# The Mixer's first levels issued ahead of its attention, whose 24 steps begin one in each slot

## The reference, cut to what matters

```
# differential attention: 6 heads, 4 blocks of 128 queries each: 24 steps
s = q_blk @ k^T  (two maps m of 32 channels);  p = softmax(s - slope * |i - j|)
a = p[0] - lam * p[1];   o = a @ v;   lam = exp(lq1 . lk1) - exp(lq2 . lk2) + lambda_init

# gated delta rule: 6 heads, both directions, chunks of 64 tokens
solve (I + strict_lower(kb k^T * decay)) [u, w] = [v*beta, kb*exp(gc)]
for each chunk:  v_new = u_i - w_i @ S;  o = qg_i @ S + aqk_i @ v_new
                 S = S * gl_i + kdec_i^T @ v_new
```

## Time and profile before

| what | value |
|---|---|
| median of 3 runs | 3787.8 us (3787.16 to 3788.26) |
| the profiled execution | 3787.34 us |
| its span on the core | 3785.6 us |
| TensorE busy | 3650.9 us, 96% |
| VectorE, ScalarE, GpSimd busy | 57%, 41%, 9% |
| granted clock of TensorE, mean | 0.986 |

### The profile page before, as it was taken

How to read it: one execution, slowest core, us unless ns; L and a number is a source line. 1 busy time by engine, 2 the same in 40 slices (tenths; PEclk the granted TensorE clock), 3 DMA queues, 4 the chain that set the end, 5 groups by cost and what they waited for, 6 DMA issues and landing times. The chain is left out here.

```text
span 3785.6 us, 58644 instructions
## 1 busy us (share of the span) xinstructions
PE 3650.9 (96%) x24913; PEld 3014.9 (80%) x24913; DVE 2164.9 (57%) x3353; ACT 1537.3 (41%) x2423; POOL 337.5 (9%) x325
## 2 busy tenths in 40 slices
PE   7999899999999999999999998999999999999998
PEld 4887688888888888878888776777888777778887
DVE  4734766455466444474227766745377866644375
ACT  3224632111354322253226435643266436633364
POOL 0030220000000000000000005510000014400000
PEclk9999899999999999999999998999999999999999
DMA  5530013333212111122223311013232311022231
GB/s 194 179 105 5 7 46 112 123 123 123 86 62 78 64 56 54 65 89 89 92 86 100 102 45 43 19 47 99 87 103 89 91 51 26 19 83 84 89 101 67
DMA packets 262767, 301.24 MB, mean 80 GB/s; under 512 B 9371, under 2 KB 229426, under 8 KB 262514
## 3 DMA queue, kind: packets, MB, share of 16 engines
q1 hardware_dynamic: 260433, 293.41, 24.2%
q10 hardware_dynamic: 2080, 4.19, 0.3%
HBM read 284.14 MB, written 2.10 MB: 76 GB/s over the span
## 5 line engine op out<-in xcount | busy, mean ns | idle before, releaser
L536 PE MATMUL banks<-h_halves,w_halves 128*128 128x512 f32 x3708 | 1370.4, 370 | 14.2 <-DVEq L428 10.6
L538 PE MATMUL banks<-h_halves,w_halves 128*128 128x512 f32 x3708 | 1364.7, 368 | 0.0
L540 PE MATMUL banks<-h_halves,w_halves 128*128 128x512 f32 x3708 | 1359.5, 367 | 0.0
L536 PEld LDWEIGHTS banks<-h_halves,w_halves 128*128 128x128 f32 x3708 | 699.0, 189 | 146.3 <-issue 13.9
L540 PEld LDWEIGHTS banks<-h_halves,w_halves 128*128 128x128 f32 x3708 | 697.3, 188 | 119.2
L538 PEld LDWEIGHTS banks<-h_halves,w_halves 128*128 128x128 f32 x3708 | 698.6, 188 | 115.6 <-issue 1.4
L263 DVE TENSOR_TENSOR w_halves<-work,w_halves 128x2048 fp32r<-128x2048 f32 (+1 forms) x212 | 482.8, 2277 | 484.9 <-ACT w_halves L258 484.9
L258 ACT ACTIVATE w_halves<-work 128x2048 fp32r<-128x2048 f32 (+1 forms) x212 | 401.8, 1895 | 387.1 <-PE banks L540 363.4
L258 ACT ACTIVATE h_halves<-kept 128x512 fp32r<-128x512 f32 (+1 forms) x520 | 332.9, 666 | 281.4 <-PE banks L540 235.6
L263 DVE TENSOR_TENSOR h_halves<-kept,h_halves 128x512 fp32r<-128x512 f32 (+1 forms) x514 | 356.9, 736 | 137.0 <-ACT h_halves L258 135.8
L1130 DVE SCALAR_TENSOR_TENSOR kept<-kept 128x512 f32<-128x512 f32 x280 | 189.8, 751 | 10.3 <-DMA kept<-in_mod_w 10.3
(11 more groups left out here) (415 smaller groups left out, 4693.0 us busy)
## 6 DMA issues: line engine op xcount, KB each, us to landing
work<-in_w_ff SPq DMA_DIRECT2D x64, 1024.0 KB, 5.3
work<-in_ffn_w_in SPq DMA_DIRECT2D x44, 1024.0 KB, 5.0
kept<-in_mod_w SPq DMA_DIRECT2D x40, 1024.0 KB, 5.2
work<-in_odd_w_in SPq DMA_DIRECT2D x24, 1024.0 KB, 5.2
work<-in_w_in SPq DMA_DIRECT2D x24, 1024.0 KB, 5.2
work<-in_ffn_w_out SPq DMA_DIRECT2D x16, 1024.0 KB, 5.2
work<-in_even_w_in SPq DMA_DIRECT2D x13, 1024.0 KB, 5.4
work<-in_odd_w_out SPq DMA_DIRECT2D x8, 1024.0 KB, 5.1
```

The lines of the kernel that those rows point to most:

```text
L536: nc.tensor.matmul(o, low[:, k - a, fc], rh[:, tc], start=opens, stop=False, skip_group_check=shared)
L538: nc.tensor.matmul(o, high[:, k - a, fc], rl[:, tc], start=False, stop=False, skip_group_check=shared)
L540: mm = nc.tensor.matmul(o, high[:, k - a, fc], rh[:, tc], start=False, stop=(k == K - 1), skip_group_check=shared)
```

## The change

The list `begins` holds the slot in which each step starts: 2, 3, ... 25, one a slot. So lags 0 to 4 of five steps stand in one slot, from slot 6 to 25; the last `weigh` is in slot 29. `scores(0)`, its wait for the stack and the 14 holds behind it go from ahead of TensorE's loop; 4 holds come into each of slots 1 to 4. In TensorE's `attend` and in ScalarE's loop the work of the older step (`weigh`, `out`) now comes ahead of that of the younger one (`turn_step` part 0, its copy). On VectorE `lambdas` and the memsets come ahead of `update(0, 0)`, and `query_gram(0)`, `lambdas_difference` and `queries(0, d)` move from ahead of the loop into slots 1, 2 and 3. `results_of_states` moves from level 5 to level 6, except in the last seven slots.

```diff
+    begins = [2 + s for s in range(N)]
+
     def step_at(t, lag):
 
-        s, odd = divmod(t + 2 - lag, 2)
-        return s if odd == 0 and 0 <= s < N else None
+        return begins.index(t - lag) if t - lag in begins else None
...
-                    if lv == 5:
+                    if lv == (6 if h < H else 5):
                         results_of_states(h - 1)
...
                 if place == 0:
-                    for s, work in ((step_at(t, 3), lambda s: turn_step(s, 0)), (step_at(t, 4), weigh)):
+                    for s, work in ((step_at(t, 4), weigh), (step_at(t, 3), lambda s: turn_step(s, 0))):
...
             pe.wait_ge(v_copied, 3)
-            pe.wait_ge(loads_in, 96)
-            scores(0)
-            core.hold(7, 14)
...
+                    if 0 < t < 5:
+                        core.hold(7, 4)
                     if h < H and lv:
                         products(h, lv)
...
-            exps(0)
             for t in range(slots):
...
                     rescale(step_at(t, 2))
+                if step_at(t, 4) is not None:
+                    out(step_at(t, 4))
                 if step_at(t, 3) is not None:
                     copy(step_at(t, 3), 0)
-                if step_at(t, 4) is not None:
-                    out(step_at(t, 4))
...
-            update(0, 0)
             dve.wait_ge(loads_in, 96)
             lambdas()
             for u in pl.u:
                 nc.vector.memset(c4(u[HD:P, 0:512])[:, :, 0:HD], 0.0)
                 nc.vector.memset(c4(u[0:HD, 512:1024])[:, :, HD:P], 0.0)
-            top(0)
-            lambdas_difference()
-            query_gram(0)
-            for d in range(2):
-                queries(0, d)
+            update(0, 0)
...
+                if t == 1:
+                    query_gram(0)
+                    lambdas_difference()
+                if t in (2, 3):
+                    queries(0, t - 2)
```

## The result

| | median us | runs | mean clock of the runs |
|---|---|---|---|
| before, beside it | 3788.26 | 3787.16 to 3788.92 | |
| changed | 3813.33 | 3805.05 to 3823.38 | 0.979 to 0.985 |

I had forecast 3776 with a range to 3791.

The account below looks back on a forecast made before the run. TensorE's own order of work was taken as the bound. Opening, packed heads, bare heads and close summed to 214.4 us a layer, 215.9 with half clock, against 222.86 and 220.89: 12 us gained, 3776 us, range 3763 to 3791.

Parts of the forecast that it names:

- The packed slots: Slots 7 to 27, heads 1 to 3, each carrying a whole attention step: 42.3 us a head, taken as 43.0.
- the new wait: In packed slots TensorE's transposes wait for the previous step's out: 0.5 us a slot, 3.5 us a head.
- the chain over VectorE and ScalarE: From one update to the next in packed slots, 5.0 to 6.2 us; overtakes TensorE at levels 1, 2, 4, 5: 1.7 us a head.
- 1.5 us for one stretch at half clock in head 0: Allowance added to each Mixer stage for TensorE's low clock in head 0, taking 214.4 to 215.9 us.
- my own 214.4: Forecast us of one Mixer stage, all parts from opening to close summed, before the 1.5 us for half clock.
- the falling clock: Rival: a third of heads 4, 5 and closing slots at low clock, 4.9 us a stage, total 3785; chance 0.24.
- 2.56 / 6.5: Price of low clock from head 0's two layers: 6.5 us more of it cost 2.56, some 0.37 each.
- The bare slots: From slot 30 on, no step fills TensorE's waits: head 4 24.8 us, head 5 17.5, plus 1.0 for both.
- the close: Last seven slots without steps, a filler between operations: 28.51 us becomes 16.9.
- Opening: Slots 0 to 6, no wait for the stack: 41.3 us become 26.4; first two updates 3.8 us apart, not 13.8.
- In packed slots it changes nothing: results_of_states moved to level 6: no gain in packed slots, whose waits are covered; about 1 us saved in bare ones.

Follow-up runs that it names:

- run 5: Changed kernel with weigh's result in PSUM bank 1, so the transposes need not wait for the earlier step's out: 3785.99 us, ratio 0.9993 to the kernel before.
- run 7: Changed kernel with two holds (about 0.35 us) between weigh and the transposes in slots that have a weigh: 3800.73 us, ratio 1.0043 to the kernel before.
- run 11: The changed kernel itself measured again, unaltered, in six runs: median 3819.74 us, ratio 1.0086 to the kernel before.
- run 6: Changed kernel with four holds (about 0.7 us) between weigh and the transposes in slots that have a weigh: 3818.39 us, ratio 1.0077 to the kernel before.
- run 8: Changed kernel with weigh's result in its own bank and two holds ahead of products in slots 30 to 41 except level 0: 3770.20 us, ratio 0.9956.
- run 3: Changed kernel with results_of_states back in level 5 and steps spread (slots 2 to 6, then every second to 44): 3785.78 us, ratio 0.9993.
- run 1: Kernel before with only results_of_states moved one slot later (level 6, except in the last seven slots): 3780.22 us, ratio 0.9973.
- run 4: Changed kernel with results_of_states put back in level 5 and nothing else: 3847.37 us, ratio 1.0159 to the kernel before.

## Why the prediction was wrong

**The packed slots: right.** 43.0 us a head was forecast from 37.1 of work, 3.5 for the new wait and 1.7 for the chain over VectorE and ScalarE; 42.08 and 41.93 were measured near full clock. The wait was 0.81 us where I had 0.5 and 0.24; run 5 took it away and the head fell to 36.95, so it cost 5.1 us a head, of my 5.2. That the sum fits so closely is in part luck: 37.1 was to be TensorE's bare work, and the 36.95 still has 2 us in which TensorE is not busy (34.97). Only head 2 was forecast too short, by 2 us, at 45.21 in run 7: it has split(2), for which I had nothing.

**The step that failed: "1.5 us for one stretch at half clock in head 0".** The stage had 69 and 33 us of it in the profiled execution, 28 and 13 us at 0.40, where I took 1.5. The same step made the comparison crooked: before, with 31 and 22 us at half clock, carries 12 and 9 us of such cost in its 222.86 and 220.89, and I set a sum at nearly full clock against it. At full clock before would be about 210.4 and 212 us a layer at 0.40, or 212.6 and 213.6 at run 11's 0.33 (estimates), and my own 214.4 was already longer. The whole forecast gain of 12 us was clock that I had given away for nothing. I had named the falling clock as a rival, with 20 us a layer in the bare and closing slots, and priced it at 2.56 / 6.5, which is 0.39 and not the 0.37 that I wrote; it fell in the packed heads too, where I had reckoned TensorE full and had myself added the idle that is shown to let it fall: runs 6 and 7 fill that idle and runs 5 and 8 remove it, and in the profiles of all four heads 1 to 3 run at 1.00 in both layers, while both profiles of the changed kernel have them at 0.77 to 0.90 in layer 0 and at 0.89 to 1.00 in layer 1. Over the whole, the median is 37 us above my 3776. The lengths at full clock, below, account for about 7 us a layer of it; the other 11 a layer are what is left for the clock (an estimate by subtraction).

The Trainium skill (TensorE: Matmul & The Clock Gate, A second HAM failure mode: psum-queue depth-cycling) tells of a kernel in which TensorE idled so briefly and so often between groups of matmuls that its clock went up and down. The rows agree in kind: the clock fell in the middle of layer 1's packed heads, at about 3215 us, after a stretch in which TensorE had been busy in 2.16 of 3.50 us; the idle was one wait for out, of 1.34 us. Not every such wait is followed by a fall: another of 1.34 us, up to 3260.69, left the clock at 1.00.

```profile
3211.50:3215.00 3.50, 2.16 (x31) 1.95 (x30) 0.97 (x3) 2.86 (x8) 0.00 (x0) 1.00 0.00 0
3215.00:3225.40 10.40, 9.95 (x76) 7.75 (x74) 4.64 (x14) 4.96 (x14) 3.64 (x4) 0.51 0.01 2
```

**The bare slots and the close: too short.** At full clock head 4 took 27.28 (forecast 24.8), head 5 19.16 (17.5, and 1.0 for both), the close 19.29 (16.9, reckoned to a slightly earlier end). Together about 5 to 6 us a layer. I had walked TensorE's own waits level by level and had only counted VectorE's and ScalarE's work there, not followed it. That this hid the difference is my guess; it was not tried.

**Opening: right in its slots, wrong in its worth.** The first two updates were 4.02 us apart (3.8 forecast) and nothing waited for the stack. Head 0 took 29.82 us at 0.87, which is 26.7 at full clock against 25.8. But the steps that it sheds come back later, so alone the opening moved the total by 2 us (run 3), with a ratio that is not clear of 1.

**results_of_states: wrong.** "In packed slots it changes nothing", and of before nothing was said. It was worth 0.6 to 1.45 us a head there (run 1) and 1.1 in a packed head, and without it the clock fell further (run 4). That in level 6 it stands in a wait that I had taken as covered is my reading; no run separates it.

**What stays open.** Put together for a layer, from the rows at full clock: 26.7 + 42.1 + 45.2 + 41.9 + 27.3 + 19.2 + 19.3 = 221.7 (head 2 as in run 7), 8 to 11 us above before at full clock, by the two prices of a us at half clock. Two layers of that, 16 to 22, and what the clock costs more than in before make the 25 us of the median; the split between the two is uncertain by a few us. Run 7 bears it out: with two holds and little half clock it is 15 us above before. Why head 2 of layer 0 has 24 us at half clock in both profiled executions and head 2 of layer 1 only 10 and 4, in the same program, no run here tells; nor why head 5 of one layer falls and that of the other not. And 7 to 13 us at half clock in head 0 stayed in every version with the new opening.

## What to carry to other kernels

Before two schedules are compared, bring both to one clock: work out the time at half clock from PEclk, price it from runs of one kernel, and ask of every wait that a change adds or uncovers on TensorE whether the clock will fall in it. A matmul that nobody needs, in a wait that nothing else fills, can make a program faster; the same matmul where TensorE has work makes it slower. Where a younger step must wait for an older step's last read of a shared PSUM bank, look for a bank of its own: here it took 27 us off, and two fillers in the wait 13. Another order of issue in the packed slots was not tried.

## What the runs showed of the hardware that I had not expected

A us at half clock cost 0.33 to 0.40 us over the whole, and in head 2 less: 2.56 us for 10.5 (47.77 at 0.89 against 45.21 at 1.00), 7.57 for 24.3 (52.78 at 0.77), 0.24 and 0.31 for each. If all of it were TensorE work that takes twice as long at 1.2 as at 2.4 GHz, it would be 0.5. I had not expected that a small idle costs a second time: 0.81 us in each of seven slots cost 4.5 to 5.1 us a head directly (run 5 against 42.08, 45.21 and 41.93), and 2.6 to 7.6 us more in head 2, where the clock fell. One program's runs spread over 18 and 20 us, in the order of their clocks.
